# Second expert table of a decoder step: the order of the weight splits in DVE's slots, gate blocks and activations in more buffers, and the final residual sum

## The chip, the cores and the metric

The kernel runs on one core of one Trainium2 chip. The metric is device time in microseconds, the median of the runs. A profiled execution of the kernel gives the rows below. TensorE (PE) does the matrix products, VectorE (DVE) and ScalarE (ACT) the element-wise work, GpSimd (POOL) issues the gathers by index, SyncE (SP) issues the other loads.

## What is computed

One step of a decoder layer for 512 prompt tokens and 32 sample tokens, D = 2048: modulation, an RWKV-7 and an RG-LRU mixer, a layer norm, and a PEER expert layer with 16384 experts, of which each token picks 8 x 16:

```python
def _peer(h, w_q, sub_keys, peer_u, peer_v):
    ...
        act = jax.nn.gelu(jnp.einsum('thkd,td->thk', peer_u[e], xb))
        return jnp.einsum('thk,thkd->td', gate * act, peer_v[e])
...
    x = _layernorm(ALPHA * x + (1 + g2) * ff, lp['ln2_w'], lp['ln2_b'])
```

## The kernel before

The program is a row of phases, each a block with a list of instructions per engine, ordered by semaphores that are written by hand. The change lies in the last two, `phase_down` (the second expert table, `peer_v`) and `phase_final` (residual sum and layer norm).

The expert layer is done densely for the first 384 tokens (TD) and by gathered rows for the other 160 picks (PICKS): the first table (`phase_up`) leaves an activation z of 128 experts x 384 tokens for each of 128 activation numbers `a` and, in 16 blocks, the gates of 8 of them each, in HBM. In `phase_down`, PE walks 128 weight tiles `v` (1 MB of `peer_v` each, 2048 columns), 8 to a group of 8 activations. A tile is 16 products of 128x128 by 384 columns, and each is done as three matmuls of reduced-precision floats (`product`, L92 to L94): operands are split into a high half and a low half, high x high + high x low + low x high. So a tile is 48 matmuls.

Who does what, per tile or slot `v`:
- SP loads the weight tile `v+2` into WR (two buffers, L1914) when the low half of tile `v` is made, and one activation z into ZI (two buffers, L1899). Once a group it loads a gate block into GG (one buffer, L1904) when the last product with the block before is done.
- ACT makes the high half of a weight tile, WH (`high`, L1948; two buffers, so it waits until PE has used the tile two before), and the high half of a gated activation, BH (`split`, L1953).
- DVE makes the low half of a weight tile, WL (`low`, L1985: WR - WH, waits for `high`), multiplies z by its gate into AF (`gated`, L1994), makes the low half of the gated activation, BL (`rest`, L2001: AF - BH, waits for `split`), adds PE's two banks of a tile to the sum YA (`collect`, L2013), and adds gathered rows times their coefficient to YS or YR (`row`, L2019; 160 rows in 128 slots, so every fourth slot has two).
- POOL gathers the rows, 1 MB each, into a ring of three (L1974), each when the row three before is added.
- PE (`v_tile`, L1923) waits for the low half of its tile, for free banks, and at a group's first tile for the low halves of the group's activations one by one.

ACT's slot `v` is `split(8+v)`, then `high(v+2)`. DVE's is:

```python
                if JG + v - 1 < NK:
                    rest(JG + v - 1)
                if v + 1 < NV:
                    low(v + 1)
                if v:
                    collect(v - 1)
                for j in range(PICKS * v // NV, PICKS * (v + 1) // NV):
                    row(j)
                if JG + v < NK:
                    gated(JG + v)
```

In `phase_final` PE turns YS (16 transposes, L2058) and sums YR (L2063), ACT copies both into the last columns of YA (L2076, L2079), DVE multiplies YA by the gate (L2093, L2095) and adds ALPHA times x (L2100), and PE forms the mean over the features (L1309) as those rows come.

Of the kernel before, what the change touches and what calls it, by code (L numbers as in the profile page):

```python
# [38 lines left out]
NK = 128  # L39
# [1830 lines left out]

ROW_RING = 3


def phase_down(nc, io, g, stack):
# [3 lines left out]
    PS, YA, YS, YR, CF, EI, WR, WH, WL = (g[x] for x in ("PS", "YA", "YS", "YR", "CF", "EI", "WR", "WH", "WL"))  # L1878
    GG = m.sb("GG", [P, TD, JG])
    ZI = m.sb("ZI", [P, 2, TD])  # L1880
    AF = m.sb("AF", [P, 2, TD])
# [3 lines left out]
    w_in, w_base = g["W_IN"], 8 * KT + 8 * (NQ + NK)  # L1885
    z_in, v_in = m.sems("z_in", 2), g["V_GOT"]
    (g_in, gg_free, hi_ready, lo_ready, used, a_ready, bh_ready, bl_ready, ya_ready, bank_free, vr_free,
     cleared) = (m.sem(x) for x in (
        "g_in gg_free hi_ready lo_ready used a_ready bh_ready bl_ready ya_ready bank_free vr_free cleared").split())
    NV = 8 * NG  # L1890

    with nc.Block() as block:
        @block.sync
        def _(sp):
            def load_z(a):

                if a >= 2:
                    sp.wait_ge(a_ready, a - 1)
                sp.dma_start(ZI[:, a % 2], io["z"][a]).then_inc(z_in[a % 2], 16)  # L1899

            def load_gates(gi):
                if gi:
                    sp.wait_ge(gg_free, gi)
                sp.dma_start(GG[:], io["gd"][gi]).then_inc(g_in, 16)  # L1904

            load_gates(0)
            for a in range(JG):
                load_z(a)
            load_gates(1)
            load_z(JG)  # L1910
            for v in range(NV):
                if v + 2 < NV:
                    sp.wait_ge(lo_ready, v + 1)
                    sp.dma_start(WR[:, v % 2, :], io["peer_v"][v + 2]).then_inc(w_in[v % 2], 16)  # L1914
                a = JG + v + 1
                if a < NK:
                    if a % JG == 0:
                        load_gates(a // JG)
                    load_z(a)

# [21 lines left out]
        def _(act):  # L1942
# [25 lines left out]

        @block.gpsimd
# [10 lines left out]
        def _(dve):  # L1980
# [6 lines left out]
            def gated(a):  # L1987

                if a % JG == 0:
                    dve.wait_ge(g_in, 16 * (a // JG) + 16)  # L1990
                dve.wait_ge(z_in[a % 2], 16 * (a // 2) + 16)
                if a >= 2:
                    dve.wait_ge(bl_ready, a - 1)
                V.tensor_tensor(AF[:, a % 2], ZI[:, a % 2], GG[:, :, a % JG], ALU.mult).then_inc(a_ready, 1)  # L1994
                if a % JG == JG - 1:
                    dve.drain().then_inc(gg_free, 1)
# [7 lines left out]
            def collect(v):  # L2004

                c = v % 8
                for ct in range(2):
                    if ct == 0:
                        dve.wait_ge(ya_ready, v + 1)
                    else:  # L2010
                        dve.wait_ge(used, v + 1)
                    y = YA[:, 2 * c + ct, 0:TD]
                    V.tensor_tensor(y, y, PS[:, (2 * c + ct) % 8, 0:TD], ALU.add).then_inc(bank_free, 1)  # L2013
# [7 lines left out]

            V.memset(YA[:, :, 0:TD], 0.0)
# [22 lines left out]
def phase_final(nc, io, g, stack):  # L2045
# [4 lines left out]
    norm = Norm(nc, m, g, XT, "ln2_w", "ln2_b")  # L2050
    x_ready, y_out, ys_done, ys_read = (m.sem(x) for x in ("x_ready", "y_out", "ys_done", "ys_read"))
    x_in = m.sems("x_in", 4)

    with nc.Block() as block:
        @block.tensor
        def _(pe):
            for kt in range(KT):
                mm = nc.tensor.transpose(PS[:, kt // 4, P * (kt % 4):P * (kt % 4) + P], YS[:, P * kt:P * kt + P], IDENT[:])  # L2058
                if kt % 4 == 3:
                    mm.then_inc(ys_done, 1)  # L2060
# [11 lines left out]
        @block.scalar  # L2072
        def _(act):
            for q in range(4):
                act.wait_ge(ys_done, q + 1)
                nc.scalar.activation(YA[:, 4 * q:4 * q + 4, TD:SEQ], PS[:, q, :].rearrange("p (k t) -> p k t", k=4),  # L2076
                                     ACT.Copy).then_inc(ys_read, 1)
            act.wait_ge(ys_done, 5)
            nc.scalar.activation(YA[:, :, SEQ:T], PS[:, 4, :].rearrange("p (k t) -> p k t", k=KT),  # L2079
                                 ACT.Copy).then_inc(ys_read, 1)  # L2080
            norm.scalar(act)

        @block.vector
        def _(dve):
# [5 lines left out]
            norm.start(dve)  # L2090
            dve.wait_ge(ys_read, 5)
            for kt in range(KT):
                V.tensor_scalar(YA[:, kt, 0:SEQ], YA[:, kt, 0:SEQ], MOD[:, 5 * KT + kt, 0:1], None, ALU.mult)  # L2093
            ys = YA[:, :, SEQ:T].rearrange("p k (b s) -> p k b s", s=NS)
            V.tensor_tensor(ys, ys, bcast(MOD[:, 5 * KT:6 * KT, 1:9], 3, NS), ALU.mult)  # L2095
# [147 lines left out]
```

## Time and profile before

| | us |
|---|---|
| runs | 4988.44, 4991.70, 4993.56 |
| median | 4991.7 |
| profiled execution, its own time | 4987.92 |
| its span | 4986.1 |
| PE busy | 4420.4 (89%) |
| PE's weight loads, beside its products | 4056.5 (81%) |
| DVE busy | 2955.7 (59%) |
| ACT busy | 1146.6 (23%) |
| POOL busy | 1058.4 (21%) |

Times in rows are counted from the start of the span. Busy shares are averages over phases that differ; the second table runs from about 3594 to 4913, the final phase from there to the end. In a row of idle time, "<-" names what ended it.

### The profile page before, as it was taken

How to read it: one execution, taken by the hardware profiler on the slowest of the kernel's cores; microseconds unless marked ns; L12 is line 12 of the kernel's file. 1: busy time of each engine (PE TensorE's matmuls, PEld its weight loads, DVE VectorE, ACT ScalarE, POOL GpSimd, SP SyncE). 2: the span in 40 equal slices, each digit the busy share in tenths (PEclk: the TensorE clock that was granted, in tenths of full speed). 3: DMA queues.
4: the chain of work that ended last, by engine and by line, in shares of the span. 5: the costliest groups of instructions: out<-in, count | busy, mean ns of one | idle time of the engine just before them, and what ended most of it. 6: DMA issues, size and time to landing. Idle time of an engine off the chain costs nothing. (4 is left out here: it accounts for less than half of the span.)

```text
span 4986.1 us, 69611 instructions
## 1 busy us (share of the span) xinstructions
PE 4420.4 (89%) x28073; PEld 4056.5 (81%) x28073; DVE 2955.7 (59%) x4235; ACT 1146.6 (23%) x1507; POOL 1058.4 (21%) x695
## 2 busy tenths in 40 slices
PE   5997888889889777969999999999898988888887
PEld 4776767777767667949999999999888888888886
DVE  1233343434344443249967878888677777777776
ACT  0222211211111111132223232232222222222222
POOL 0000111211211120033453333333212222212220
PEclk7998988888889778979999999999999999999998
DMA  8221212222211214212348999998877777777773
GB/s 337 70 70 70 70 59 81 71 76 67 78 66 42 75 60 152 76 64 84 109 146 334 335 344 331 334 334 330 305 268 252 279 262 277 265 275 265 275 269 148
DMA packets 208668, 923.58 MB, mean 185 GB/s; under 512 B 20960, under 2 KB 105056, under 8 KB 109152
## 3 DMA queue, kind: packets, MB, share of 16 engines
q1 hardware_dynamic: 91104, 526.16, 28.8%
q0 software_dynamic: 49408, 344.48, 19.1%
q10 hardware_dynamic: 67968, 50.34, 3.0%
q8 instruction: 130, 2.13, 0.2%
q14 instruction: 58, 0.48, 0.0%
HBM read 854.62 MB, written 66.28 MB: 185 GB/s over the span
## 5 line engine op out<-in xcount | busy, mean ns | idle before, releaser
L92 PE MATMUL PS<-first_HH,tail_WH 128*128 128x384 f32 (+1 forms) x3072 | 1004.9, 327 | 41.8 <-DVE first_HL L1487 31.9
L93 PE MATMUL PS<-first_HL,tail_WH 128*128 128x384 f32 (+1 forms) x3072 | 987.7, 322 | 0.0
L94 PE MATMUL PS<-first_HH,tail_WL 128*128 128x384 f32 (+1 forms) x3072 | 985.7, 321 | 0.0
L92 PE MATMUL PS<-dn_BH,tail_WH 128*128 128x384 f32 x2048 | 720.1, 352 | 173.4 <-DVE tail_WL L1985 94.3
L93 PE MATMUL PS<-dn_BL,tail_WH 128*128 128x384 f32 x2048 | 708.9, 346 | 0.0
L94 PE MATMUL PS<-dn_BH,tail_WL 128*128 128x384 f32 x2048 | 708.9, 346 | 0.0
L92 PEld LDWEIGHTS PS<-first_HH,tail_WH 128*128 128x128 f32 x3072 | 580.8, 189 | 44.4 <-issue 38.3
L93 PEld LDWEIGHTS PS<-first_HL,tail_WH 128*128 128x128 f32 x3072 | 580.8, 189 | 0.5
L94 PEld LDWEIGHTS PS<-first_HH,tail_WL 128*128 128x128 f32 x3072 | 579.7, 189 | 0.0
L92 PEld LDWEIGHTS PS<-dn_BH,tail_WH 128*128 128x128 f32 x2048 | 403.0, 197 | 202.4 <-issue 135.3
L1974 POOL DMA_INDIRECT dn_VR<-in_v_rows,tail_EI x160 | 266.1, 1663 | 1054.9 <-DVEq L2020 1015.7
L1758 POOL DMA_INDIRECT up_UR<-in_u_rows,tail_EI x160 | 344.2, 2151 | 613.7 <-DVEq L1852 586.5
L712 PE MATMUL PS<-mix_HT,mix_RING 128*128 128x276 f32 x1536 | 383.0, 412 | 48.8 <-DMA mix_RING<-in_w_in 24.6
L1985 DVE TENSOR_TENSOR tail_WL<-tail_WR,tail_WH 128x2048 fp32r<-128x2048 f32 x128 | 293.4, 2292 | 193.6 <-ACT tail_WH L1948 193.6
L712 PEld LDWEIGHTS PS<-mix_HT,mix_RING 128*128 128x128 f32 x1536 | 303.4, 199 | 124.6 <-issue 25.6
L93 PEld LDWEIGHTS PS<-dn_BL,tail_WH 128*128 128x128 f32 x2048 | 404.3, 197 | 0.0
L94 PEld LDWEIGHTS PS<-dn_BH,tail_WL 128*128 128x128 f32 x2048 | 402.9, 197 | 0.0
L1832 DVE TENSOR_TENSOR tail_WL<-tail_WR,tail_WH 128x2048 fp32r<-128x2048 f32 x104 | 238.4, 2293 | 185.6 <-ACT tail_WH L1680 183.6
L1850 DVE SCALAR_TENSOR_TENSOR up_UR<-up_UR,first_XS 128x2048 f32<-128x2048 f32 x128 | 293.5, 2293 | 15.3
L2019 DVE SCALAR_TENSOR_TENSOR last_YS<-dn_VR,tail_CF,last_YS 128x2048 f32<-128x2048 f32 x128 | 300.4, 2347 | 3.0
L1953 ACT ACTIVATE dn_BH<-dn_AF 128x384 fp32r<-128x384 f32 x128 | 67.2, 525 | 937.1 <-DVE dn_AF L1994 937.1
L1680 ACT ACTIVATE tail_WH<-tail_WR 128x2048 fp32r<-128x2048 f32 x144 | 274.8, 1909 | 4.2 <-PEq L130 2.1
(365 smaller groups left out, 6374.6 us busy)
## 6 DMA issues: line engine op xcount, KB each, us to landing
tail_WR<-in_peer_u SPq DMA_DIRECT2D x128, 1024.0 KB
tail_WR<-in_peer_v SPq DMA_DIRECT2D x128, 1024.0 KB
mix_RING<-in_w_ada SPq DMA_DIRECT2D x96, 1024.0 KB, 4.9
mix_RING<-in_w_in SPq DMA_DIRECT2D x42, 1024.0 KB, 4.9
tmp_z<-up_ZB ACTq DMA_DIRECT2D x128, 192.0 KB
tmp_gd<-up_STG ACTq DMA_DIRECT2D x24, 1024.0 KB
dn_GG<-tmp_gd SPq DMA_DIRECT2D x16, 1536.0 KB
dn_ZI<-tmp_z SPq DMA_DIRECT2D x128, 192.0 KB, 4.0
```

What stands on the lines that cost most here:

```text
L92: nc.tensor.matmul(out, r32(wh), r32(xh), start=first, stop=False)
L93: nc.tensor.matmul(out, r32(wh), r32(xl), start=False, stop=False)
L94: return nc.tensor.matmul(out, r32(wl), r32(xh), start=False, stop=last)
L712: mm = nc.tensor.matmul(PS[:, BANKS[which] + half, 0:TPH], RING[:, which, P * kt:P * kt + P], HT[:, kt, TPH * half:TPH * half + TPH], star ...
L1680: A(r32(WH[:, i % 2]), WR[:, i % 2], ACT.Copy).then_inc(hi_ready, 1)
L1758: pool.indirect_dma_start(UR[:, j % DOT_RING, :], None, io["u_rows"], bass.IndirectOffsetOnAxis(EI[:, j:j + 1], 0)).then_inc(u_in[j % DOT_ ...
L1832: V.tensor_tensor(r32(WL[:, i % 2]), WR[:, i % 2], WH[:, i % 2], ALU.subtract).then_inc(lo_dve, 1)
L1850: V.scalar_tensor_tensor(row, row, 1.0, (XS if j < P else XR)[:], ALU.mult, ALU.mult, accum_out=ZS[:, j:j + 1])
L1953: A(r32(BH[:, (a // JG) % 2, a % JG, :]), AF[:, a % 2], ACT.Copy).then_inc(bh_ready, 1)
L1974: pool.indirect_dma_start(VR[:, j % ROW_RING, :], None, io["v_rows"], bass.IndirectOffsetOnAxis(EI[:, j:j + 1], 0)).then_inc(v_in[j % ROW_ ...
L1985: V.tensor_tensor(r32(WL[:, v % 2]), WR[:, v % 2], WH[:, v % 2], ALU.subtract).then_inc(lo_ready, 1)
L2019: V.scalar_tensor_tensor(y, VR[:, j % ROW_RING, :], CF[:, j:j + 1], y, ALU.mult, ALU.add)
```

## The change

DVE's slot makes the low half of the weight tile first and then the low half of an activation, one activation later than before: one more `gated` stands ahead of the loop, and slot `v` ends with `gated(9+v)` instead of `gated(8+v)`. ACT's slot is `high(v+2)`, then `split(9+v)`. ZI has four buffers and GG two. YA holds the 384 dense tokens only. In `phase_final` the sample sums go into a tile of their own (SS), ACT multiplies x by ALPHA in four passes, and DVE adds gate times YA, and gate times the turned YS straight from PSUM, to it.

```diff
+Z_RING = 4
...
-    GG = m.sb("GG", [P, TD, JG])
-    ZI = m.sb("ZI", [P, 2, TD])
+    GG = m.sb("GG", [P, 2, TD, JG])
+    ZI = m.sb("ZI", [P, Z_RING, TD])
...
             def load_z(a):
 
-                if a >= 2:
-                    sp.wait_ge(a_ready, a - 1)
-                sp.dma_start(ZI[:, a % 2], io["z"][a]).then_inc(z_in[a % 2], 16)
+                if a >= Z_RING:
+                    sp.wait_ge(a_ready, a - Z_RING + 1)
+                sp.dma_start(ZI[:, a % Z_RING], io["z"][a]).then_inc(z_in[a % Z_RING], 16)
 
             def load_gates(gi):
-                if gi:
-                    sp.wait_ge(gg_free, gi)
-                sp.dma_start(GG[:], io["gd"][gi]).then_inc(g_in, 16)
+                if gi >= 2:
+                    sp.wait_ge(gg_free, gi - 1)
+                sp.dma_start(GG[:, gi % 2], io["gd"][gi]).then_inc(g_in[gi % 2], 16)
 
             load_gates(0)
-            for a in range(JG):
+            for a in range(Z_RING):
                 load_z(a)
             load_gates(1)
-            load_z(JG)
+            for a in range(Z_RING, JG + Z_RING):
+                load_z(a)
+            load_gates(2)
             for v in range(NV):
                 if v + 2 < NV:
                     sp.wait_ge(lo_ready, v + 1)
                     sp.dma_start(WR[:, v % 2, :], io["peer_v"][v + 2]).then_inc(w_in[v % 2], 16)
-                a = JG + v + 1
-                if a < NK:
-                    if a % JG == 0:
-                        load_gates(a // JG)
-                    load_z(a)
+                if JG + Z_RING + v < NK:
+                    load_z(JG + Z_RING + v)
+                if v % JG == JG - 1 and v // JG + 3 < NG:
+                    load_gates(v // JG + 3)
...
             high(1)
+            split(JG)
             for v in range(NV):
-                if JG + v < NK:
-                    if v % JG == 0 and v:
-
-                        act.wait_ge(used, v)
-                    split(JG + v)
                 if v + 2 < NV:
                     act.wait_ge(used, v + 1)
                     high(v + 2)
+                if JG + v + 1 < NK:
+                    split(JG + v + 1)
...
-            for a in range(JG):
+            for a in range(JG + 1):
                 gated(a)
                 if a:
                     rest(a - 1)
             for v in range(NV):
-                if JG + v - 1 < NK:
-                    rest(JG + v - 1)
                 if v + 1 < NV:
                     low(v + 1)
+                if JG + v < NK:
+                    rest(JG + v)
                 if v:
                     collect(v - 1)
                 for j in range(PICKS * v // NV, PICKS * (v + 1) // NV):
                     row(j)
-                if JG + v < NK:
-                    gated(JG + v)
+                if JG + v + 1 < NK:
+                    gated(JG + v + 1)
...
+            act.wait_ge(ss_done, 1)
+            nc.scalar.activation(SS[:], PS[:, 4, :].rearrange("p (k t) -> p k t", k=KT), ACT.Copy).then_inc(ss_read, 1)
             for q in range(4):
...
+                act.wait_ge(x_in[q], 16)
+                nc.scalar.activation(XT[:, 4 * q:4 * q + 4, :], XT[:, 4 * q:4 * q + 4, :], ACT.Copy,
+                                     scale=ALPHA).then_inc(x_scaled, 1)
...
+            V.tensor_tensor(ss, ss, bcast(MOD[:, 5 * KT:6 * KT, 1:9], 3, NS), ALU.mult)
+            dve.drain()
             for kt in range(KT):
...
+                gate = MOD[:, 5 * KT + kt, 0:1]
                 if kt % 4 == 0:
...
+                    dve.wait_ge(x_scaled, kt // 4 + 1)
+                    xs = XT[:, kt:kt + 4, SEQ:T]
+                    V.tensor_tensor(xs, xs, SS[:, kt:kt + 4], ALU.add)
+                V.scalar_tensor_tensor(XT[:, kt, 0:TD], YA[:, kt, :], gate, XT[:, kt, 0:TD], ALU.mult, ALU.add)
+                dve.wait_ge(ys_done, 4 * (kt // 4) + 4)
+                V.scalar_tensor_tensor(XT[:, kt, TD:SEQ], PS[:, kt // 4, P * (kt % 4):P * (kt % 4) + P], gate,
+                                       XT[:, kt, TD:SEQ], ALU.mult, ALU.add).then_inc(x_ready, 1)
```

In the instruction lists (engine left out; line, operation, out<-in, elements) this shows first on DVE, in a slot with one row early in the second table. Line numbers are those of each kernel. Before:

```order
L2001 TENSOR_TENSOR dn_BL<-dn_AF,dn_BH 128x384
L1985 TENSOR_TENSOR tail_WL<-tail_WR,tail_WH 128x2048
L2013 TENSOR_TENSOR last_YA<-last_YA,PS 128x384 x2
L2019 SCALAR_TENSOR_TENSOR last_YS<-dn_VR,tail_CF,last_YS 128x2048
L1994 TENSOR_TENSOR dn_AF<-dn_ZI,dn_GG 128x384
```

And now:

```order
L1985 TENSOR_TENSOR tail_WL<-tail_WR,tail_WH 128x2048
L2001 TENSOR_TENSOR dn_BL<-dn_AF,dn_BH 128x384
L2013 TENSOR_TENSOR last_YA<-last_YA,PS 128x384 x2
L2019 SCALAR_TENSOR_TENSOR last_YS<-dn_VR,tail_CF,last_YS 128x2048
L1994 TENSOR_TENSOR dn_AF<-dn_ZI,dn_GG 128x384
```

The low half of the weights (L1985) has moved ahead of the low half of an activation (L2001). ACT's list has the same rows in the same order in both kernels (eight splits, then high and split in turn); the split behind a given high is that of the activation one later.

The second place is SP at the start of the second table. Before:

```order
L1904 DMA dn_GG<-tmp_gd 128x3072
L1899 DMA dn_ZI<-tmp_z 128x384 x8
L1904 DMA dn_GG<-tmp_gd 128x3072
L1899 DMA dn_ZI<-tmp_z 128x384
L1914 DMA tail_WR<-in_peer_v 128x2048
```

And now:

```order
L1905 DMA dn_GG<-tmp_gd 128x3072
L1900 DMA dn_ZI<-tmp_z 128x384 x4
L1905 DMA dn_GG<-tmp_gd 128x3072
L1900 DMA dn_ZI<-tmp_z 128x384 x8
L1905 DMA dn_GG<-tmp_gd 128x3072
L1917 DMA tail_WR<-in_peer_v 128x2048
```

The second gate block goes out after four activations instead of eight, and a third one stands ahead of the first weight load of the phase.

The third place is DVE in the final phase. Before:

```order
L2093 TENSOR_SCALAR last_YA<-last_YA,all_MOD 128x512 x16
L2095 TENSOR_TENSOR last_YA<-last_YA,all_MOD 128x16x32
L2100 SCALAR_TENSOR_TENSOR last_XT<-last_XT,last_YA 128x544 x16
```

And now, to the end of the second of 16 feature tiles:

```order
L2093 TENSOR_TENSOR fin_SS<-fin_SS,all_MOD 128x512
L2100 TENSOR_TENSOR last_XT<-last_XT,fin_SS 128x4x32
L2101 SCALAR_TENSOR_TENSOR last_XT<-last_YA,all_MOD,last_XT 128x384
L2103 SCALAR_TENSOR_TENSOR last_XT<-PS,all_MOD,last_XT 128x128
L2101 SCALAR_TENSOR_TENSOR last_XT<-last_YA,all_MOD,last_XT 128x384
L2103 SCALAR_TENSOR_TENSOR last_XT<-PS,all_MOD,last_XT 128x128
```

The 16 multiplications by the gate ahead of the sum are gone, and each feature tile's sum is two operations.

## Rows read from the trace of the kernel before

**Rows 1.** Windows: first table, then second; columns in the first line.
```profile
core 0: us, PE busy (x) PEld busy (x) DVE busy (x) ACT busy (x) POOL busy (x), PEclk, DMA share, GB/s
2700.00:3300.00 600.00, 600.00 (x3609) 600.00 (x3608) 479.22 (x585) 180.73 (x195) 216.22 (x99) 1.00 0.91 335
3609.00:4912.00 1303.00, 1148.62 (x6144) 1119.66 (x6144) 958.86 (x797) 298.14 (x254) 263.23 (x157) 0.95 0.73 265
```

**Rows 2.** Timeline of ACT, last tiles: start, us, engine, line, operation, [idle before <-releaser].
```profile
4869.92 1.92 ACT L1948 ACTIVATE tail_WH<-tail_WR 128x2048 fp32r<-128x2048 f32 x1 [6.40 <-PE PS L94]
4878.24 1.92 ACT L1948 ACTIVATE tail_WH<-tail_WR 128x2048 fp32r<-128x2048 f32 x1 [6.40 <-PE PS L94]
```

**Rows 3.** Timeline of PE: first product of tiles 0 and 1, last product.
```profile
3609.33 0.66 PE L92 MATMUL PS<-dn_BH,tail_WH 128*128 128x384 f32 x1 [19.89 <-DVE dn_BL L2001]
...
3626.48 0.33 PE L92 MATMUL PS<-dn_BH,tail_WH 128*128 128x384 f32 x1
...
4911.15 0.34 PE L94 MATMUL PS<-dn_BH,tail_WL 128*128 128x384 f32 x1
```

**Rows 4.** Groups by line, second table: xcount | busy us, mean ns | idle before <-releasers.
```profile
L92 PE MATMUL PS<-dn_BH,tail_WH 128*128 128x384 f32 x2048 | 720.1, 352 | 173.4 <-DVE tail_WL L1985 94.3 <-DVE dn_BL L2001 78.8 <-issue 0.2
```

**Rows 5.** Timeline of DVE, one slot, and the end of the two-row slot behind it.
```profile
3636.87 0.91 DVE L1994 TENSOR_TENSOR dn_AF<-dn_ZI,dn_GG 128x384 f32<-128x384 f32 x1 [0.19 <-issue]
3638.38 0.56 DVE L2001 TENSOR_TENSOR dn_BL<-dn_AF,dn_BH 128x384 fp32r<-128x384 f32 x1 [0.59 <-ACT dn_BH L1953]
3640.18 2.29 DVE L1985 TENSOR_TENSOR tail_WL<-tail_WR,tail_WH 128x2048 fp32r<-128x2048 f32 x1 [1.25 <-ACT tail_WH L1948]
3642.39 1.01 DVE L2013 TENSOR_TENSOR last_YA<-last_YA,PS 128x384 f32<-128x384 f32 x2
3643.32 2.35 DVE L2019 SCALAR_TENSOR_TENSOR last_YS<-dn_VR,tail_CF,last_YS 128x2048 f32<-128x2048 f32 x1
3645.85 0.91 DVE L1994 TENSOR_TENSOR dn_AF<-dn_ZI,dn_GG 128x384 f32<-128x384 f32 x1 [0.19 <-issue]
...
3657.31 0.92 DVE L1994 TENSOR_TENSOR dn_AF<-dn_ZI,dn_GG 128x384 f32<-128x384 f32 x1 [0.19 <-issue]
```

**Rows 6.** Timeline of ACT in the same slot.
```profile
3637.82 0.53 ACT L1953 ACTIVATE dn_BH<-dn_AF 128x384 fp32r<-128x384 f32 x1 [6.65 <-DVE dn_AF L1994]
3638.25 1.90 ACT L1948 ACTIVATE tail_WH<-tail_WR 128x2048 fp32r<-128x2048 f32 x1
```

**Rows 7.** Gated products: a wait at the start and at a group, and the total.
```profile
3610.31 0.85 DVE L1994 TENSOR_TENSOR dn_AF<-dn_ZI,dn_GG 128x384 f32<-128x384 f32 x1 [1.13 <-DMA dn_ZI<-tmp_z]
...
3709.01 0.92 DVE L1994 TENSOR_TENSOR dn_AF<-dn_ZI,dn_GG 128x384 f32<-128x384 f32 x1 [4.62 <-DMA dn_ZI<-tmp_z]
...
  DMA dn_ZI<-tmp_z: 51.8, 19
```

**Rows 8.** Timeline of SP: the weight load ahead of rows 6.
```profile
3633.52 0.33 SPq L1914 DMA_DIRECT2D tail_WR<-in_peer_v  x1
```

**Rows 9.** POOL's gathers, and us from their issue to landing.
```profile
4312.46 2.99 POOL L1974 DMA_INDIRECT dn_VR<-in_v_rows,tail_EI  x1 [7.35 <-DVEq L2020]
4315.76 0.94 POOL L1974 DMA_INDIRECT dn_VR<-in_v_rows,tail_EI  x1 [0.30 <-issue]
...
DMA to landing us min/median/max: 5.4/7.3/12.0
```

**Rows 10.** Final phase: x loads, the mean, and operations of the new shapes elsewhere.
```profile
4913.38 2.14 SPq L2108 DMA_DIRECT2D last_XT<-tmp_x  x4
...
DMA to landing us min/median/max: 5.1/8.5/11.7
...
4927.52 17.79 PE PS L1309 x64
...
L1447 ACT ACTIVATE first_HH<-out_MIX 128x2176 fp32r<-128x2176 f32 x4 | 8.1, 2017 | 7.9 <-DMA out_MIX<-tmp_mix 7.9
L1217 DVE TENSOR_TENSOR rw_SB<-rw_K,PS 128x128 f32<-128x128 f32 x128 | 36.8, 288 | 150.6 <-PE PS L762 143.7 <-issue 6.9
```

More of the change, by code:

```diff
@@ L1885, in phase_down @@
     w_in, w_base = g["W_IN"], 8 * KT + 8 * (NQ + NK)
-    z_in, v_in = m.sems("z_in", 2), g["V_GOT"]
-    (g_in, gg_free, hi_ready, lo_ready, used, a_ready, bh_ready, bl_ready, ya_ready, bank_free, vr_free,
+    z_in, g_in, v_in = m.sems("z_in", Z_RING), m.sems("g_in", 2), g["V_GOT"]
+    (gg_free, hi_ready, lo_ready, used, a_ready, bh_ready, bl_ready, ya_ready, bank_free, vr_free,
      cleared) = (m.sem(x) for x in (
-        "g_in gg_free hi_ready lo_ready used a_ready bh_ready bl_ready ya_ready bank_free vr_free cleared").split())
+        "gg_free hi_ready lo_ready used a_ready bh_ready bl_ready ya_ready bank_free vr_free cleared").split())
     NV = 8 * NG
@@ L1989, in gated @@
                 if a % JG == 0:
-                    dve.wait_ge(g_in, 16 * (a // JG) + 16)
-                dve.wait_ge(z_in[a % 2], 16 * (a // 2) + 16)
+                    dve.wait_ge(g_in[a // JG % 2], 16 * (a // JG // 2) + 16)
+                dve.wait_ge(z_in[a % Z_RING], 16 * (a // Z_RING) + 16)
                 if a >= 2:
                     dve.wait_ge(bl_ready, a - 1)
-                V.tensor_tensor(AF[:, a % 2], ZI[:, a % 2], GG[:, :, a % JG], ALU.mult).then_inc(a_ready, 1)
+                V.tensor_tensor(AF[:, a % 2], ZI[:, a % Z_RING], GG[:, a // JG % 2, :, a % JG], ALU.mult).then_inc(a_ready, 1)
                 if a % JG == JG - 1:
@@ L2011, in collect @@
                         dve.wait_ge(used, v + 1)
-                    y = YA[:, 2 * c + ct, 0:TD]
+                    y = YA[:, 2 * c + ct, :]
                     V.tensor_tensor(y, y, PS[:, (2 * c + ct) % 8, 0:TD], ALU.add).then_inc(bank_free, 1)
@@ L2020, in row @@
                 dve.drain().then_inc(vr_free, 1)
-            V.memset(YA[:, :, 0:TD], 0.0)
+            V.memset(YA[:], 0.0)
             V.memset(YS[:], 0.0)
@@ L2050, in phase_final @@
     norm = Norm(nc, m, g, XT, "ln2_w", "ln2_b")
-    x_ready, y_out, ys_done, ys_read = (m.sem(x) for x in ("x_ready", "y_out", "ys_done", "ys_read"))
+    SS = m.sb("SS", [P, KT, NR4])
+    x_ready, y_out, ys_done, ss_done, ss_read, x_scaled = (m.sem(x) for x in (
+        "x_ready y_out ys_done ss_done ss_read x_scaled").split())
     x_in = m.sems("x_in", 4)
@@ L2056, in _ @@
         def _(pe):
[L2057 to L2060, printed above, removed]
             pe.wait_ge(sum4_ready, 1)
@@ L2064, in _ @@
                                       start=True, stop=True)
-            mm.then_inc(ys_done, 1)
+            mm.then_inc(ss_done, 1)
+            for kt in range(KT):
+                nc.tensor.transpose(PS[:, kt // 4, P * (kt % 4):P * (kt % 4) + P], YS[:, P * kt:P * kt + P],
+                                    IDENT[:]).then_inc(ys_done, 1)
             pe.wait_ge(norm.ones_ready, 1)
-            pe.wait_ge(ys_read, 5)
+            pe.wait_ge(ss_read, 1)
             for kt in range(KT):
@@ L2073, in _ @@
         def _(act):
+            act.wait_ge(ss_done, 1)
+            nc.scalar.activation(SS[:], PS[:, 4, :].rearrange("p (k t) -> p k t", k=KT), ACT.Copy).then_inc(ss_read, 1)
             for q in range(4):
[L2075 to L2080, printed above, removed]
+                act.wait_ge(x_in[q], 16)
+                nc.scalar.activation(XT[:, 4 * q:4 * q + 4, :], XT[:, 4 * q:4 * q + 4, :], ACT.Copy,
+                                     scale=ALPHA).then_inc(x_scaled, 1)
             norm.scalar(act)
@@ L2090, in _ @@
             norm.start(dve)
[L2091 to L2095, printed above, removed]
+            dve.wait_ge(ss_read, 1)
+            ss = SS[:].rearrange("p k (b s) -> p k b s", s=NS)
+            V.tensor_tensor(ss, ss, bcast(MOD[:, 5 * KT:6 * KT, 1:9], 3, NS), ALU.mult)
             dve.drain()
             for kt in range(KT):
+                gate = MOD[:, 5 * KT + kt, 0:1]
                 if kt % 4 == 0:
-                    dve.wait_ge(x_in[kt // 4], 16)
-                V.scalar_tensor_tensor(XT[:, kt, :], XT[:, kt, :], ALPHA, YA[:, kt, :], ALU.mult, ALU.add)\
-                    .then_inc(x_ready, 1)
+                    dve.wait_ge(x_scaled, kt // 4 + 1)
[5 more added lines that the diff above has]
+                                       XT[:, kt, TD:SEQ], ALU.mult, ALU.add).then_inc(x_ready, 1)
             dve.drain()
@@ L2132, in phase_rest @@
         last = Mem(nc, tail, "last")
-        g.update({"YA": last.sb("YA", [P, KT, T]), "YS": last.sb("YS", [P, D]), "YR": last.sb("YR", [P, D])})
+        g.update({"YA": last.sb("YA", [P, KT, TD]), "YS": last.sb("YS", [P, D]), "YR": last.sb("YR", [P, D])})
         run(phase_down, nc, io, g)
```

## Prediction

> **What bounds the kernel now.** I read the windows by stage first, to find a stage where TensorE is not full. In the first expert table (2700 to 3300) PE is busy 600.00 of 600 us at a granted clock of 1.00; in the second (3609 to 4912) it is busy 1148.62 of 1303 at 0.95 [rows 1]. So the second table is where time can be won, and PE's own pace there is the floor. The last tiles give that floor: ACT's high half starts each time when PE ends a tile, at 4869.92 and 4878.24, so a tile of 48 matmuls takes 8.32 us [rows 2]. 128 tiles are 1065.0 us, while the stage runs from 3609.33 to 4911.15 + 0.34, 1302.2 us [rows 3]. Of the 237.2 us between, 173.4 are idle time before the first product of a group, put down to the low half (L1985) and the low half of an activation (L2001) [rows 4]; the other 64 are products at the half clock (the granted clock of the stage is 0.95, against 1.00 where PE is full [rows 1]), which follows the gaps.
>
> Next comes the order of time of one slot, to see why the low half is late. On DVE: gated at 3636.87, rest 3638.38, low 3640.18, collect 3642.39, row 3643.32, next gated 3645.85 [rows 5]. On ACT: split at 3637.82, high at 3638.25 for 1.90 us [rows 6]. This is a ring: gated (0.95 to the split), split (0.43), high (1.93), low (2.21), collect (0.93), row (2.53), gated again. It closes in 8.98 us, and in 11.46 where a slot has two rows (3645.85 to 3657.31): ACT's high half stands behind a split that waits for the gated product at the end of DVE's slot. Four slots take 3 x 8.98 + 11.46 = 38.4 us where PE needs 33.3. On top, gated waits 4.62 us once a group for the single gate block or an activation (in all 51.8 us, 19 times) [rows 7].
>
> **The change, part by part.**
>
> *The order in the slots.* ACT's list of rows is the same before and after; what moves is DVE's. Before, DVE does gated(8+v), rest(8+v), low(v+2); now gated(9+v), low(v+2), rest(9+v), with one more gated ahead of the loop. ACT's split ahead of high(v+2) is then that of a product made a slot earlier, so high(v+2) waits only for the end of PE's tile v. Let tile v+1 start at 0: high runs 0 to 1.9, low 1.96 to 4.2, and it is needed at 8.32: 4.1 us to spare. DVE's slot is 2.21 + 0.56 + 0.93 + 2.53 + 0.91 = 7.14 us, with two rows 2.48 more, 9.62 [rows 5]; four are 31.0 of PE's 33.3, 93%. A two-row slot ends 3.26 into the next tile, its low half is then done at 5.47, still 2.9 early, and the next slot catches up. At a group's start the last low half of an activation comes 0.56 after low, while PE reads it only as the eighth of eight. So nothing is late next: PE runs without gaps, as in the first table, and its clock with it.
> The first tile I leave as it is, 3609.33 to 3626.48 or 17.15 us [rows 3]: it is paced by DVE's start-up and runs at the half clock; there one gated more (+0.9) stands against up to four waits for z less (the longest 1.13 [rows 7]; at most -4.5). Bounds -4.5 to +0.9, taken as 0. The stage becomes 17.15 + 127 x 8.32 = 1073.8: **-228.4 us**.
>
> *Four activations, two gate blocks.* Same bytes, asked for earlier. On SP a z load now stands ahead of the next weight load and waits for gated(8+v), which DVE finishes before the low half that the weight load waits for anyway: no delay. A gate block goes ahead of a weight tile once in eight, as it did. The 51.8 us are inside the 237 above and not counted again. At the start the second gate block, 1.57 MB or 4.7 us at 335 GB/s, now goes out ahead of activation 4, which is asked for only when DVE's first gated is done, some 12 us later: no delay.
>
> *Transfers.* A tile brings 1.05 MB of weights, 0.20 of z, 0.20 of gates and 1.25 gathered MB-rows of 1.05: 2.75 MB in 8.32 us, 331 GB/s, where the stage moved 265 at a DMA share of 0.73. The first table moved 335 at 0.91 with PE full [rows 1]. So I cost it at 0. A weight tile may take 2 x 8.32 - 4.2 = 12.4 us; issued at 3633.52 it had landed by 3638.25 [rows 6, 8].
>
> *Gathered rows.* POOL takes 0.94 us to issue a gather when it starts with DVE idle (4315.76) and 2.99 when a row has just begun (4312.46): it ends 0.8 after that one DVE instruction and needs no longer rest of DVE than the 0.2 us between a row and the next gated [rows 5, 9]. It waits for one instruction, not for the train. The ring of three gives a row 2 x 8.32 - 2.5 = 14.1 us at the least, and the longest landing is 12.0 [rows 9]: 0 us, though DVE goes from 74% to 93% busy.
> The Trainium skill (SBUF — State Buffer, section "SBUF: two separate sides", the "DVE blocks DMA" trap) says that GpSimd cannot write descriptors while DVE holds the port pair they share, and that the DMA engines then sit idle. The trace agrees for single instructions (0.94 against 2.99). Read for a DVE that never rests, the rule speaks against this change, and is a rival below; by it the sum would be 67 us worse.
>
> *The final stage.* Now the mean's 64 matmuls (17.79 us) start at 4927.52, after ACT's copies, 16 multiplications, and one 544-wide row sum [rows 10]. The gate is folded into the sum, and the scaling of x goes to ACT while x lands. First x quarter: 4913.38 + 5.1 = 4918.5; a 2176-wide ACT pass, 2.02: 4920.5; on DVE the sample sum over 128 elements (0.3), a 384-wide op (0.5, half of collect's pair) and a 128-wide one from PSUM (0.3): 4921.6 [rows 5, 10]. The last quarter, issued by 4915.5, comes at 4915.5 + 11.7 + 2.0 + 3.5 = 4932.7, before PE wants it (4939). So **-5.9 us**; 0 if the x quarters came late; I keep the mean's 17.79, of which a higher clock could give back half at most, -14.8. The rest of the stage is untouched.
>
> **Sum.** -228.4 - 5.9 = -234.3 against the profiled execution, 4987.92: 4753.6. The median of the runs shown is 3.8 above that execution, so **4757 us**.
>
> **The rivals.**
> *Transfers become the bound.* For it: 331 GB/s is all but what the first table moved, at a share of 0.91. Against: PE was full there, with more gathered rows per us. It decides where a weight tile lands after 12.4 + 2.9 = 15.3 us. At 320 GB/s a tile takes 8.60: +36, 4793; at 300, 9.18: +109, 4866.
> *DVE becomes the bound.* At 93% a wait of 0.6 a slot makes it so. If the 1.25 us wait for the high half stayed in every slot, a slot is (31.0 + 5.0) / 4 = 9.0: +86, 4843. Against: the ring through gated and split is cut.
> *Descriptors held back.* If a gather issued in a full DVE slot had to wait the slot out, 12.0 + 7.1 = 19.1 against 14.1 + 2.9 to spare, 2.1 late in one tile of four: 32 x 2.1 = +67, 4824. Against: the 2.99 rows, where POOL got in between two instructions.
> *It does not do what it says.* ACT's list is unchanged, so if DVE's order did not matter either, only the final stage gains: 4986.
> *Slower.* The ring of gathered rows is the place. Today 160 rows pass in 1302 us, 24.4 us for three; if landing plus use went over that, every slot would wait, and DVE's low half with it. At a landing of 24, (24 + 2.5) / 3 x 160 = 1413: +111 in the stage, -6 in the last: 5097. It takes landings three times those seen (7.3 in the middle, 12.0 at most), under a load that the first table carried.
>
> **How the numbers follow.** Forecast 0.79; transfers 0.11; DVE 0.04; descriptors 0.02; no effect 0.02; slower 0.02. A measurement of this kernel tells about 0.2%, 10 us. Faster by more: 0.79 + 0.11 + 0.04 + 0.02 = 0.96; within: 0.02; slower: 0.02. The forecast's own range is 4745 (part of a faster mean, z waits -4.5, spread of the runs) to 4770 (first weight tiles behind the gate block, the final stage unchanged); with the nearer part of the transfer case it is 4745 to 4795.
>
> **What would show it.** Right: in the stage PE without idle time after the first tile, granted clock near 1.00, ACT's high half 8.32 apart throughout, DVE's idle time before the low half about 1 us in one-row slots and none after two-row ones, about 331 GB/s at 0.9, no wait of gated for a DMA after the first group; stage 1074 us; the mean's first product 8.2 us after the final stage's first x load is issued (14.1 before). Wrong: ACT waiting for weights in most slots (transfers), DVE without any idle time and PE waiting for L1985's successor (DVE), rows waiting for gathers (descriptors).

## The result, and the profile after

The changed kernel takes **4754.58 us** (median of four runs, 4748.55 to 4757.06), where the kernel before takes 4992.63 in the same comparison: a ratio of 0.9523, 95% interval 0.9506 to 0.9539. The forecast was 4757.0. The profiled execution took 4756.15 us, its span 4754.1; against 4987.92 that is -231.8, where the sum said -234.3.

The windows of after by stage (columns as in [rows 1]): the second table, its steady part, and the final phase.

```profile
3609.00:4687.00 1078.00, 1072.75 (x6144) 1068.87 (x6144) 948.49 (x797) 301.67 (x253) 338.58 (x157) 0.99 0.84 320
3660.00:4600.00 940.00, 940.00 (x5425) 940.00 (x5424) 841.51 (x707) 268.78 (x226) 309.18 (x141) 1.00 0.87 330
4687.00:4754.00 67.00, 41.06 (x176) 32.87 (x176) 40.77 (x76) 31.89 (x39) 0.00 (x0) 0.78 0.33 134
```

PE, which had 1148.62 busy us in 1303 at 0.95 [rows 1], is now busy for 940.00 of 940 at 1.00. DVE is at 90% there and the transfers run at 330 GB/s, against 93% and 331 forecast. The group that held 173.4 us of idle time [rows 4] holds 23.0, of which 19.9 stand ahead of the stage's first product:

```profile
L92 PE MATMUL PS<-dn_BH,tail_WH 128*128 128x384 f32 x2048 | 687.5, 336 | 23.0 <-DVE dn_BL L2001 22.5
```

ACT's timeline in the middle of the stage, where the high half now starts on PE's end and the split behind it is done long before the next one:

```profile
4218.97 1.92 ACT L1950 ACTIVATE tail_WH<-tail_WR 128x2048 fp32r<-128x2048 f32 x1 [5.99 <-PE PS L94]
4222.19 0.53 ACT L1955 ACTIVATE dn_BH<-dn_AF 128x384 fp32r<-128x384 f32 x1 [1.30 <-DVE dn_AF L1994]
4227.29 1.92 ACT L1950 ACTIVATE tail_WH<-tail_WR 128x2048 fp32r<-128x2048 f32 x1 [4.57 <-PE PS L94]
```

The two high halves are 8.32 apart, PE's own pace in [rows 2]. In [rows 6] the high half came right behind a split that had waited 6.65 for the gated product; now ACT has stood idle for 5.99 or 4.57 us when PE frees the buffer. DVE's timeline over the same time, a two-row slot and the one behind it:

```profile
4212.60 2.29 DVE L1985 TENSOR_TENSOR tail_WL<-tail_WR,tail_WH 128x2048 fp32r<-128x2048 f32 x1 [1.27 <-ACT tail_WH L1950]
4214.81 0.55 DVE L2001 TENSOR_TENSOR dn_BL<-dn_AF,dn_BH 128x384 fp32r<-128x384 f32 x1
4215.28 1.01 DVE L2013 TENSOR_TENSOR last_YA<-last_YA,PS 128x384 f32<-128x384 f32 x2
4216.21 4.82 DVE L2019 SCALAR_TENSOR_TENSOR last_YS<-dn_VR,tail_CF,last_YS 128x2048 f32<-128x2048 f32 x2
4221.24 0.92 DVE L1994 TENSOR_TENSOR dn_AF<-dn_ZI,dn_GG 128x384 f32<-128x384 f32 x1 [0.22 <-issue]
4222.07 2.29 DVE L1985 TENSOR_TENSOR tail_WL<-tail_WR,tail_WH 128x2048 fp32r<-128x2048 f32 x1
...
4229.24 2.29 DVE L1985 TENSOR_TENSOR tail_WL<-tail_WR,tail_WH 128x2048 fp32r<-128x2048 f32 x1
```

The low half waits 1.27 us in a slot that is early and not at all behind a two-row slot (4212.60 to 4222.07, 9.47), and the next slot takes 7.17 and catches up. That is the picture that the prediction asked for, within 0.2 us a slot. In the waits of the second table, PE's are left at the start alone, and gated waits for a transfer twice, where it did 19 times for 51.8 us [rows 7]:

```profile
DVE tail_WL L1985 <- ACT tail_WH L1950: 93.1, 74, 2.9
...
PE PS L92 <- DVE dn_BL L2001: 22.5, 4, 19.9
...
DVE dn_AF L1994 <- DMA dn_ZI<-tmp_z: 2.4, 2, 1.9
```

PE's first product of tiles 0 and 1 and its last product, as in [rows 3]:

```profile
3608.91 0.66 PE L92 MATMUL PS<-dn_BH,tail_WH 128*128 128x384 f32 x1 [19.89 <-DVE dn_BL L2001]
...
3628.05 0.33 PE L92 MATMUL PS<-dn_BH,tail_WH 128*128 128x384 f32 x1
...
4684.51 0.34 PE L94 MATMUL PS<-dn_BH,tail_WL 128*128 128x384 f32 x1
```

The stage takes 1075.9 us, from the first product at 3608.91 to 4684.85 (1302.2 before, 1073.8 forecast); the rest of the gain is nearly all in the final phase.

### The profile page after: what moved, and what is told of

Same layout as the page of the kernel before. It is cut to its first block and busy times, and to the rows that moved or that the text cites. A ratio compares the mean times of both kernels' runs of the same rounds, so it can differ in the third digit from the quotient of the medians.

```text
span 4754.1 us, 69606 instructions
## 1 busy us (share of the span) xinstructions
PE 4350.0 (91%) x28073; PEld 4008.7 (84%) x28073; DVE 2941.9 (62%) x4239; ACT 1155.8 (24%) x1507; POOL 1134.0 (24%) x695
## 5 line engine op out<-in xcount | busy, mean ns | idle before, releaser
L92 PE MATMUL PS<-dn_BH,tail_WH 128*128 128x384 f32 x2048 | 687.5, 336 | 23.0 <-DVE dn_BL L2001 22.5
L94 PE MATMUL PS<-dn_BH,tail_WL 128*128 128x384 f32 x2048 | 686.1, 335 | 0.0
L93 PE MATMUL PS<-dn_BL,tail_WH 128*128 128x384 f32 x2048 | 686.1, 335 | 0.0
L1974 POOL DMA_INDIRECT dn_VR<-in_v_rows,tail_EI x160 | 341.4, 2134 | 753.4 <-DVEq L2020 718.1
L1950 ACT ACTIVATE tail_WH<-tail_WR 128x2048 fp32r<-128x2048 f32 x128 | 245.9, 1921 | 718.0 <-PE PS L94 707.8
L92 PEld LDWEIGHTS PS<-dn_BH,tail_WH 128*128 128x128 f32 x2048 | 385.8, 188 | 26.8 <-issue 20.2
L93 PEld LDWEIGHTS PS<-dn_BL,tail_WH 128*128 128x128 f32 x2048 | 386.1, 189 | 0.0
L94 PEld LDWEIGHTS PS<-dn_BH,tail_WL 128*128 128x128 f32 x2048 | 386.0, 188 | 0.0
L1985 DVE TENSOR_TENSOR tail_WL<-tail_WR,tail_WH 128x2048 fp32r<-128x2048 f32 x128 | 293.4, 2292 | 95.4 <-ACT tail_WH L1950 93.1
L1680 ACT ACTIVATE tail_WH<-tail_WR 128x2048 fp32r<-128x2048 f32 x144 | 274.8, 1909 | 4.2 <-PEq L130 2.1
```

Source lines behind the costliest of these rows:

```text
L92: nc.tensor.matmul(out, r32(wh), r32(xh), start=first, stop=False)
L93: nc.tensor.matmul(out, r32(wh), r32(xl), start=False, stop=False)
L94: return nc.tensor.matmul(out, r32(wl), r32(xh), start=False, stop=last)
L1680: A(r32(WH[:, i % 2]), WR[:, i % 2], ACT.Copy).then_inc(hi_ready, 1)
L1950: A(r32(WH[:, v % 2]), WR[:, v % 2], ACT.Copy).then_inc(hi_ready, 1)
L1974: pool.indirect_dma_start(VR[:, j % ROW_RING, :], None, io["v_rows"], bass.IndirectOffsetOnAxis(EI[:, j:j + 1], 0)).then_inc(v_in[j % ROW_ ...
```

## The experiments

Five theories. **A**, the prediction's: the ring through gated, split and high bound the slot, and making each product one slot ahead cuts it. **B**: the buffers did it, the order is ornament. **C**: what counts is the low half ahead of the low half of the activation. **D**: DVE is now the bound, or all but. **E**: the transfers are. Each kernel was compared with the kernel before; medians in us, ratio with its 95% interval. Four kernels undo or split the change, four load it, three go on from it.

### One part alone: the order (e1_order_only)

```diff
 (before; ACT)   for a in range(JG): split(a) ... high(1)
+                split(JG)
 (loop)          high(v + 2)
+                if JG + v + 1 < NK: split(JG + v + 1)   # was split(JG + v), ahead of high
 (DVE)
-                rest(JG + v - 1); low(v + 1); collect; row; gated(JG + v)
+                low(v + 1); rest(JG + v); collect; row; gated(JG + v + 1)
```

ACT's edit only writes its loop in another way: its list is the same, activation for activation, in both kernels (high(v+2) stands between split(8+v) and split(9+v) before and after). So what moves is DVE's list alone.

> The change's order of DVE's and ACT's slots, with the buffers of before (two activations, one gate block) and the final phase of before. Theory A (the ring gated, split, high, low is what cost the time, and making each gated product one slot earlier cuts it): nearly the whole gain is here. The single gate block still comes late once a group, by 0 to 3 us, which the 2.9 to 4.1 us that the low half now has to spare take up: stage 1075 to 1090 us, and 5 us more than the change for the old final phase: 4760 to 4775 us. Theory B (the single gate block and the two activations are what hold DVE and through it PE): at most a third of the gain, over 4900 us. Theory C (what counts is only that the low half of the weights stands ahead of the low half of an activation): as A here.

Measured: **4771.96** (4769.96 to 4775.47), 0.9574 [0.9558, 0.959]. With one gate block and two activations every tile but the first takes 8.32 us. The first takes 25.4, for the first row below, of DVE's timeline (the ninth gated product; SP issued the second gate block at 3617.23 and the activation that the row names right behind it). The other two are ACT's high half in the middle of the stage, 8.32 apart as in the change:

```profile
3624.18 0.85 DVE L1992 TENSOR_TENSOR dn_AF<-dn_ZI,dn_GG 128x384 f32<-128x384 f32 x1 [6.33 <-DMA dn_ZI<-tmp_z]
```
```profile
4223.60 1.92 ACT L1948 ACTIVATE tail_WH<-tail_WR 128x2048 fp32r<-128x2048 f32 x1 [5.99 <-PE PS L94]
...
4231.92 1.92 ACT L1948 ACTIVATE tail_WH<-tail_WR 128x2048 fp32r<-128x2048 f32 x1 [4.58 <-PE PS L94]
```

The stage is 1082.2 us: the order is worth 220.0 of the 226.3 that the stage gained. B falls as the main cause.

### One part alone: the buffers and the final phase (e2_buffers_only)

```diff
 (after; ACT and DVE loops as in before)
-    low(v + 1); rest(JG + v); collect; row; gated(JG + v + 1)
+    rest(JG + v - 1); low(v + 1); collect; row; gated(JG + v)
```

SP's loads of activations and gates are moved by one slot too, to match the later product.

> Four activations, two gate blocks and the new final phase, with the slots of DVE and ACT in the order of before. Theory A: the ring stays, 38.4 us for four slots where PE needs 33.3; only the waits of gated for transfers go, and with them 82.0 - 76.8 = 5.2 us in each of 15 groups, 78 us, and 5 us in the final phase: about 4909 us (4895 to 4925). Theory B: most of the gain, 4755 to 4820 us. Theory C: as A.

Measured: **4911.88** (4907.9 to 4918.23), 0.9856 [0.984, 0.9873]. The slots are 8.98 and 11.45 us as before, the ninth 9.07; the stage is 1228.0. The waits of PE in the second table show both old names still there:

```profile
PE PS L92 <- DVE dn_BL L2003: 79.0, 19, 19.9
PE PS L92 <- DVE tail_WL L1987: 43.1, 54, 2.6
```

So alone the buffers save 74.2 us of the stage, by taking the wait of 4.62 [rows 7] and what follows it out of each group. With the order they save 6.3 (1082.2 to 1075.9): they and the order remove in part the same idle time, and the two gains must not be added.

### The order within the slot (e3_swap_only, e4_rest_first)

The first puts the low half of the weights ahead in the kernel before, with gated where it was; the second takes that step back out of the change, with gated still one ahead.

```diff
 (e3: before, DVE)
-    rest(JG + v - 1); low(v + 1); collect; row; gated(JG + v)
+    low(v + 1); rest(JG + v - 1); collect; row; gated(JG + v)
 (e4: after, DVE)
-    low(v + 1); rest(JG + v); collect; row; gated(JG + v + 1)
+    rest(JG + v); low(v + 1); collect; row; gated(JG + v + 1)
```

> The kernel before with one thing changed: in DVE's slot the low half of the weights stands ahead of the low half of an activation, and no gated product is made earlier. Theory A: the ring gated, split, high, low stays, and the low half of the activation, so far beside ACT's high half, now lies in it: 0.48 to 0.56 us more in each of some 120 slots, 58 to 67 us: 5050 to 5060 us, slower than before. Theory C: faster, the weights' low half comes 0.5 us earlier in each slot: 4930 us or less. Theory B: within 10 us of before.

Measured: **5031.02** (5029.27 to 5035.82), 1.0094 [1.0077, 1.0111]: slower by 45 us than the kernel before (4985.8 there), where A had 5050 to 5060. ACT, then DVE, in one slot:

```profile
3643.89 0.53 ACT L1953 ACTIVATE dn_BH<-dn_AF 128x384 fp32r<-128x384 f32 x1 [7.12 <-DVE dn_AF L1994]
...
3646.26 2.29 DVE L1985 TENSOR_TENSOR tail_WL<-tail_WR,tail_WH 128x2048 fp32r<-128x2048 f32 x1 [2.40 <-ACT tail_WH L1948]
3648.47 0.55 DVE L2001 TENSOR_TENSOR dn_BL<-dn_AF,dn_BH 128x384 fp32r<-128x384 f32 x1
```

DVE stands idle for 2.40 us ahead of the low half, waiting for the high half behind the split, where the rest of the activation used to fill part of that time; the slot grows by the rest's 0.47, to 9.45 and 11.92. The ninth slots, which wait for the gate block, were shorter than before (13.4 to 14.7 us from low half to low half, 13.7 in the mean, against 13.7 to 15.8, 14.3 in the mean): that is a part of the expected loss that did not come.

> The change with one thing undone: in DVE's slot the low half of an activation stands ahead of the low half of the weights again; the gated product stays one slot earlier. Theory A: the low half of the weights is 0.56 us later and had 2.9 to 4.1 to spare: no difference, 4750 to 4762 us. Theory C: most of the gain goes, over 4850 us. Theory B: no difference.

Measured: **4754.7** (4754.08 to 4759.73), 0.9539 [0.9524, 0.9555], a stage of 1076.0: the change's own time. C falls from both sides. The order of the two low halves, which the change is named after, does nothing here and harms without the product ahead.

### How full is DVE? (e5_dve_plus1, e6_dve_plus2)

```diff
 (after, DVE, in each slot, into a tile that nobody reads)
+    for d in range(1):   # e6: range(2)
+        V.tensor_tensor(DUM[:, d], DUM[:, 2], DUM[:, 2], ALU.add)
```

> The change with one more DVE operation in each of 128 slots of the second table (a sum of 384 columns into a tile that nobody reads, between the low half of an activation and collect; about 0.47 us). Theory A (PE is the bound, DVE has 31.0 us of work in four slots of 33.3): 1.9 us more in four slots is 32.9, still under PE: 4750 to 4765 us. Rival D (at 93% DVE is in truth the bound, or close enough that every wait shows): 128 x 0.3 to 0.47, 4790 to 4815 us.

Measured: **4752.45** (4747.2 to 4754.7), 0.9537 [0.9521, 0.9552]: no difference.

> As the run before with two such operations per slot, 0.94 us. Theory A: four slots are 34.8 us on DVE against 33.3 on PE, so DVE is the bound where the slots are full, about 120 of them: 0.39 us each, 45 us more: 4785 to 4815 us. Rival D: twice what the run before adds, 4830 to 4875 us.

Measured: **4777.79** (4773.45 to 4780.71), 0.9586 [0.957, 0.9602]. Windows of the two, in this order:

```profile
3660.00:4600.00 940.00, 940.00 (x5425) 940.00 (x5425) 891.66 (x820) 272.91 (x226) 320.98 (x141) 1.00 0.86 329
```
```profile
3660.00:4600.00 940.00, 924.27 (x5292) 916.16 (x5291) 913.63 (x909) 269.26 (x221) 309.65 (x138) 1.00 0.86 322
```

At 95% busy DVE costs nothing; at 97% it sets the pace. In the second kernel its low halves are 10.41, 7.90, 7.90 and 7.89 us apart, 34.1 for four and 34.3 for the next four, where PE needs 33.3. Without the eight added operations at 0.47 that is 30.3 to 30.5, not the 31.0 of the prediction, which added whole durations (rest 0.56, gated 0.91) where the next operation here starts 0.47 and 0.82 after their starts. So the change leaves DVE about 2.9 us in four tiles, and the expected 4785 to 4815 was too high for that reason. D is true only in that DVE is the next bound.

### How full are the transfers? (e7_dma_plus1, e8_dma_plus2)

```diff
 (after, SP, in each slot, into a buffer that nobody reads)
+    for d in range(1):   # e8: range(2)
+        sp.dma_start(ZX[:, v % 2, d], io["z"][v]).then_inc(zx_in[v % 2], 16)
```

> The change with one more load of 0.20 MB in each of 128 slots (an activation read again into a tile that nobody reads, on SP's queue behind the z load): 2.95 MB a tile, 354 GB/s at PE's pace. Theory A (transfers are not the bound; 330 GB/s at a DMA share of 0.87 is 379 at a full share): no difference, 4750 to 4765 us. Rival E (transfers are at the edge already): 10 us more or over, 4765 to 4790 us.

Measured: **4756.2** (4750.37 to 4757.62), 0.9544 [0.9528, 0.9559].

> As the run before with two such loads a slot: 3.15 MB a tile, 378 GB/s at PE's pace, which is what a full share would give. Theory A: at the edge; between no difference and, at 368 GB/s (335 at a share of 0.91 in the first table), 8.55 us a tile: 4755 to 4790 us. Rival E: 40 us more or over, above 4795 us.

Measured: **4757.08** (4747.39 to 4759.52), 0.9538 [0.9522, 0.9554]. Windows of the two:

```profile
3660.00:4600.00 940.00, 940.00 (x5425) 940.00 (x5424) 840.48 (x707) 268.74 (x226) 310.33 (x141) 1.00 0.91 353
```
```profile
3660.00:4600.00 940.00, 940.00 (x5425) 940.00 (x5424) 840.82 (x708) 270.00 (x227) 315.83 (x142) 1.00 0.96 377
```

With 0.39 MB more in each tile the stage moves 377 GB/s at a share of 0.96, and PE still has no idle time. The margin is nearly gone, as the waits of ACT in that window show (it had one such wait in the whole stage of the change, of 6.7 us at its start); PE's 940.00 busy us show that the longest, 7.9 us, still fits into the time that a weight tile has to spare:

```profile
ACT tail_WH L1958 <- DMA tail_WR<-in_peer_v: 55.3, 8, 7.9
```

E falls with a margin of 47 GB/s. The Trainium skill (DMA: Bandwidth & Descriptors, section "Bandwidth") gives about 358 GB/s for a core where both cores of a memory stream, and up to 425 for one alone. The 377 of this kernel, which runs on one core, lies above the first figure and below the second, as the page has it for a core alone; no run here has the other core streaming.

### Going on from the change (e9_after_again, e10_start, e11_final, e12_both)

The first is the change itself, timed beside three attempts to better it: the clearing of the sums moved from DVE to GpSimd ahead of the gathers; the small selection matrix of the final phase made at the end of the down stage, so that its sums need not wait for DVE; and both.

```diff
 (e10, GpSimd ahead of its gathers; the three V.memset of DVE gone)
+    nc.gpsimd.memset(YS[:], 0.0); nc.gpsimd.memset(YR[:], 0.0); nc.gpsimd.memset(YA[:], 0.0)
+    pool.drain().then_inc(cleared, 1)          # DVE waits for it ahead of its loop
 (e11, DVE ahead of the last sums of the down stage; SUM4 allocated beside YA, YS, YR)
+    V.tensor_copy(g["SUM4"][rows, :], g["IDENT"][rows, rows])   # four of them
 (e11, final phase)
-    pe.wait_ge(sum4_ready, 1)
```

> The change itself, once more, to stand beside the three runs of this call: 4748 to 4758 us.

Measured: **4756.2** (4747.02 to 4759.45, five runs), 0.9535 [0.9522, 0.9548].

> The change with a shorter start of the second table: the three clears of the sums (8.7 us on DVE ahead of its first low half) go to POOL, ahead of its gathers, so that DVE starts when the first gate block and activations land (3600.7 and 3603.7 in the trace of the change, with three gathers of 1 MB in the way) instead of at 3604.5. Theory: the first tile ends 4 to 8 us earlier, the rest is as it was: 4 to 8 us less than the run beside it. Rival: the first tiles wait for their weights (loaded behind the third gate block) and nothing is won.

Measured: **4748.86** (4747.75 to 4753.89), 0.9529 [0.9516, 0.9542]. The median is 7.3 lower and the intervals overlap, so the times alone do not settle it. The trace shows 3.9: from the stage's first load to its last product it is 1087.3 us (3590.82 to 4678.10) against 1091.2 in the change (3593.66 to 4684.85). DVE starts its low half 2.0 us after the stage's first load instead of 10.8, but its gated products then wait 6.9 us in all for their loads (2.4 in the change). Three of the rows:

```profile
3592.86 2.29 DVE L1989 TENSOR_TENSOR tail_WL<-tail_WR,tail_WH 128x2048 fp32r<-128x2048 f32 x1 [4.31 <-ACT tail_WH L1950]
3597.94 1.62 DVE L1998 TENSOR_TENSOR dn_AF<-dn_ZI,dn_GG 128x384 f32<-128x384 f32 x2 [2.79 <-DMA dn_ZI<-tmp_z]
...
3612.81 0.85 DVE L1998 TENSOR_TENSOR dn_AF<-dn_ZI,dn_GG 128x384 f32<-128x384 f32 x1 [1.76 <-DMA dn_ZI<-tmp_z]
```

> The change with the small matrix that sums YR made at the end of the second table, in the time in which DVE waits for PE's last tile, so that PE's first sums of the final phase need not wait 2.9 us and do not run at the half clock (7.04 us for 32 matmuls in the change, 3.66 in the kernel before). Theory: ACT's copy of the sums starts 4 us earlier, x has landed by then, and the first product of the mean comes 3 to 4 us earlier: 2 to 4 us less than the change. Rival: the pause between the sums and the mean grows, the mean runs at the half clock, and what is won is given back.

Measured: **4773.23** (4768.92 to 4774.65), 0.9573 [0.956, 0.9586]: slower than the change by 17.0 us, which no theory had.

> Both edits of the two runs before together. Theory: the sum of both, 6 to 12 us less than the change: 4740 to 4749 us.

Measured: **4770.26** (4757.95 to 4771.72), 0.9564 [0.9551, 0.9577], 14 above the change. The final phase is not where it went: from the last product to the end it takes 69.7 and 66.5 us, against 69.2. It went in the stage, in every tile, though the lists of all engines are the same there but for four small copies of DVE at its end. The windows of e11, and its group of the page that answers to the one of after above:

```profile
3660.00:4600.00 940.00, 940.00 (x5356) 940.00 (x5355) 834.04 (x700) 262.63 (x224) 309.15 (x140) 1.00 0.86 326
```
```profile
L92 PE MATMUL PS<-dn_BH,tail_WH 128*128 128x384 f32 x2048 | 693.7, 339 | 22.7 <-DVE dn_BL L2001 22.4
```

PE is busy for all of the 940 us at a granted clock of 1.00 and yet ends 5356 products instead of 5425, 1.3% fewer; a tile takes 8.43 us (8.45 with both edits), and 127 times 0.11 is 14.0. Nothing waits: the products themselves are slower (339 ns in the mean, 336 in the change). What the two kernels have in common, and no other kernel here has, is a buffer of 128 bytes a partition that is allocated ahead of the stage's own, so that activations, gates and gathered rows stand that much further on. Whether the place of the buffers is the cause was not tried and stays open. The e5 to e8 kernels also added buffers (3 kB and more a partition) and, but for e6, where DVE sets the pace, kept 8.32, but theirs are allocated behind the stage's own and move none of them; between the kernel before and the change the buffers do move, by their sizes in multiples of 1024 bytes, and PE's pace is 8.32 in both.

No kernel here beats the change by a difference that the times show; by its trace e10 does, by 3.9 us.

## Why the prediction was right

**The stage.** The floor, 8.32 us a tile, was read from the last tiles [rows 2] and is what the 127 tiles behind the first take: 127 x 8.32 stands as predicted, and e1 shows that the order alone gives it. The reason is the prediction's, the ring through gated, split and high, since the product one slot ahead decides (e4) and the swap without it harms (e3). The total of 237.2 us to be won was right, but not how it was divided: 19.9 of the 173.4 us of idle time stand ahead of the stage's first product [rows 3]. With PE busy for 1148.6 of 1302.2 us [rows 1, 3], 153.5 were idle time and some 84, not 64, were products at the half clock. The gain came in both parts, since PE now runs on at 1.00.

**The first tile** was mis-sized. The sum had 17.15 with bounds of -4.5 and +0.9; it took 19.14, 2.0 more and outside. The step that failed is "At the start the second gate block ... now goes out ahead of activation 4 ...: no delay". DVE's row for that product, and SP's for the loads:

```profile
3613.90 0.85 DVE L1994 TENSOR_TENSOR dn_AF<-dn_ZI,dn_GG 128x384 f32<-128x384 f32 x1 [1.92 <-DMA dn_ZI<-tmp_z]
```
```profile
3596.35 0.48 SPq L1905 DMA_DIRECT2D dn_GG<-tmp_gd  x1
3607.56 11.85 SPq L1900 DMA_DIRECT2D dn_ZI<-tmp_z  x8
```

The gate block, issued at 3596.35, had landed only at 3613.35, 17 us later and not 4.7: ahead of it and beside it were the first block, four loads of z and three gathers of 1 MB. From the first block's issue to that landing the transfers moved 378 GB/s at a share of 0.96. The fifth z, issued at 3607.56 behind it on SP's queue, landed at 3613.88, and the fifth gated product started on it at 3613.90. The full rate was taken for a block that shared it.

That wait is not the whole of the 2.0 us. In all, gated waited 2.4 us for z in the first tile, where it had been 2.3, so the waits that might have gone (up to 4.5 us) did not; the one gated more (the +0.9) stands ahead of the last low half of the eight; and PE's clock rose later. Before, then after, up to the product in which it rose:

```profile
3609.33:3622.38 13.05, 10.35 (x26) 7.30 (x27) 9.32 (x14) 4.94 (x7) 0.00 (x0) 0.50 0.46 134
```
```profile
3608.91:3625.30 16.39, 13.28 (x34) 9.73 (x35) 13.25 (x17) 5.35 (x8) 0.00 (x0) 0.50 0.79 288
```

PE's first product with the eighth activation came 12.4 us after the start of the tile instead of 11.8; the other 1.4 us are the products behind it, of which more ran at 0.50. How far the later clock follows from the later loads no run separates.

**The final phase** came out at -5.4 (its sum -5.9) from two misses that nearly cancel. PE's and ACT's timelines of after:

```profile
4687.77 7.04 PE L2061 MATMUL PS<-fin_SUM,last_YR 128*128 128x32 f32 x32 [2.92 <-DVEq L2089]
...
4698.61 14.91 PE L1309 MATMUL PS<-last_XT,fin_nONES 128*128 128x272 f32 x64 [0.73 <-DVE last_XT L2103]
```
```profile
4694.85 0.60 ACT L2076 ACTIVATE fin_SS<-PS 128x512 f32<-128x512 f32 x1 [24.68 <-PE PS L2061]
4695.34 7.72 ACT L2079 ACTIVATE last_XT<-last_XT 128x2176 f32<-128x2176 f32 x4
```

The mean's first product comes 11.7 us after the first x load is issued (4686.91), not 8.2 (14.1 before). The failed step is "First x quarter: ... 4918.5; a 2176-wide ACT pass": in ACT's list the copy of the sums stands ahead of that pass, and the 32 sums, now first on PE, begin 2.92 us after its last product and run for 7.04 at half the clock. So x is not what the pass waits for: its first quarter landed 5.1 us after its issue, and the pass starts 8.4 us after it. In return the mean, which followed 8.65 us of idle time before, follows 0.73 now and takes 14.91 at a granted clock of 1.00 instead of 17.79 at 0.84: the prediction named this gain and left it out of the sum. (A slip beside it: 4939 is where the mean would have ended; by its start at 4921.6, PE wants the last quarter at 4934.9, still behind the 4932.7 of the prediction.) In e1 the old final phase, with its sums at the half clock too, took 78.9 us from the last product to the end, against 69.2 in after: beside that run the new one is worth 9.7.

**The rivals.** Transfers: refuted, with 47 GB/s to spare (e8). DVE: no, but the next bound, at about 2.9 us in four tiles (e6). Descriptors held back: issuing a gather took 2134 ns in the mean, where it was 1663 before, and landing 12.3 us at most, where it was 12.0 [rows 9], and 7.7 in the middle, where it was 7.3; no row waited for a gather. With DVE 95% busy (e5) the time did not move, so nothing starved here. The trap that the Trainium skill describes (SBUF — State Buffer, section "SBUF: two separate sides") is stated there for DVE operations in a two-port mode; the longer issues agree with a wait of that kind, but no run shows in which mode these operations ran. No effect, and slower by the ring of gathered rows: neither is seen.

## What to carry to other kernels

Write the order of time of one slot as a ring across the engines; if it closes in more than the bound engine's pace, look for one operation that can be made a slot earlier, and expect the bound engine's pace, no more, once the ring is cut. Two remedies for the same idle time are not added: here the buffers were worth 74 us alone and 6 behind the order. What is bought at the full transfer rate is to be priced behind all that is already queued, at the start of a stage above all.

## What the runs showed of the hardware

- A load of 1.57 MB issued behind another of its size and four small ones, with three gathers of 1 MB beside it, landed 17.0 us after its issue (the same load ahead of them 7.0), and a load of 0.20 MB issued behind it 11 us later landed 6.3 us after its own.
- Small matmuls behind a short pause ran at either clock. The granted clock in after: 0.89 in the pause of 2.92 us, 0.50 in the sums behind it, which is the lower of the two levels (1.2 of 2.4 GHz). Before, 1.94 us of idle time and the transposes stood ahead of the same sums, which took 3.66 us at 1.00, in e3 too; in e1, with the same code and the same 1.94 us, they took 6.88 at 0.50. What decides between the two was not found.

```profile
4684.85:4687.77 2.92, 0.00 (x1) 0.00 (x1) 1.24 (x5) 0.00 (x0) 0.00 (x0) 0.89 0.00 0
4687.80:4690.50 2.70, 2.70 (x13) 2.70 (x13) 0.17 (x1) 0.00 (x0) 0.00 (x0) 0.50 0.97 316
```

- Products of one form, back to back at a granted clock of 1.00, took 1.3% longer in two kernels (e11, e12) whose instructions in the stage are those of the change; the cause is open.
